# A gMLP and sliding-window-attention trunk: the first mixer's output projection in groups two to four as seven block products

## The chip, the cores and the metric

The kernel runs on one core of a Trainium2 chip. The metric is device time of one launch in microseconds (us); lower is better. PE is the tensor engine (TensorE), DVE is VectorE, ACT is ScalarE, POOL is GpSimd and SP is SyncE, which issues nearly all transfers.

## The reference, cut to what matters

```
def mixer_a(h, w_in, ln_g, ln_b, w_s, b_s, w_out):
    u, v, z = jnp.split(h @ w_in, 3, axis=-1)          # h: 2048 x 1024, w_in: 1024 x 6144
    u = jax.nn.gelu(u)
    v = layer_norm(jax.nn.gelu(v), ln_g, ln_b)
    ...                                                 # v mixed over 128 positions, per group of 256 channels
    y = u * mixed.reshape(B, S, A_WIDTH) * jax.nn.silu(z)
    return y @ w_out                                    # y: 2048 x 2048, w_out: 2048 x 1024
...
x = x + gate * mixer_a(...)                             # then one layer of windowed attention, and a final norm
```

All is fp32. The text is about `y @ w_out`.

## The kernel before

Tokens are worked in four groups of T = 512 (`NG`, index i = 0 to 3; "group two" is i = 1). A group's part of the first mixer runs on PE in three stretches: the v columns, eight u/z stages (`GROUPS`, index g; each two units, the spatial matmuls of L2130 and four transposes of the group before), and the output projection. After the four groups comes the attention layer, in slots.

A matmul in fp32 is made of three in a rounded type (`split3`, L1930 to L1932): every operand is a rounded part and a remainder. A unit is a weight block of 4 row tiles x 512 columns, loaded by SP in two halves into one of two buffers in turn, or a third (`buffers`, L147). ScalarE rounds each half (`hi`, L1117, into `w_hi`), GpSimd subtracts (`lo`, L935, into `w_lo`). In groups two to four the v columns are already done as seven block products instead of eight (`FACTORS`, `v_blocks`), with four of the seven weight factors combined beforehand: in group one SP loads the four blocks (`load_comb`, L684), VectorE forms four sums (`comb`, L1600), ScalarE and GpSimd split them (L1140, L954), and SP stores both parts (`keep_comb`, L691), read back later as they are (`kept_split`).

The projection (`ao_unit`) has 8 units per group, each of 8 pieces: 4 token tiles x 2 pairs of rows. The y tiles are rounded by ScalarE (`y_round`, L1273) and their remainders taken by VectorE (`y_rest`, L1736); all eight PSUM banks accumulate until `a_residual` (L1588, L1590) multiplies by the gate and adds to x1. In the last unit PE also turns the next group's x (`x_transposes`).

Each engine runs its own list in the order written, with semaphore waits; nothing is reordered. The order that matters around the change is SP's: `a_stage(i, q)` with q = 4 + g issues the loads of u/z stage g, stores the split weights of two stages earlier (`keep_split`), stores a combination, loads the next and the next B weights to be split (`load_split`); after it `keep_turned` stores two turned tiles of x1. ScalarE's `turned_round` (L1180) waits for the store of the tile before. ScalarE's list in a stage is: `turned_round`, `v_norm` (L1284), `hi` of the next stage's first unit, u and z activations, `hi` of its second unit, split, combination. GpSimd's is: `lo` of both units, split, combination.

## Time and profile before

| | us |
|---|---|
| median of 3 runs | 2280.02 (2278.74 to 2284.73) |
| the profiled execution | 2281.42 |
| its span | 2279.3 |
| PE busy in the span | 2207.7 |
| granted PE clock, mean | 0.994 |

How to read the rows: times are us from the span's start. A line of the timeline gives start, duration, engine and source line, output<-inputs and the count merged; in brackets the idle time before it and what ended it. SPq is SP's own queue of DMA issues: there the duration is that of issuing, not of the transfer. Matmul durations overlap, so their spacing is their cost.

### The profile page before, as it was taken

The numbers are of one execution on the slowest core, as the hardware profiler recorded it, in microseconds if no ns is written. First come the engines' busy times: TensorE is split into PE (matmuls) and PEld (weight loads), VectorE is DVE, ScalarE is ACT, GpSimd is POOL, SyncE is SP. The second block draws the span as 40 slices with busy tenths as digits, with TensorE's granted clock in tenths as the row PEclk, the third lists the DMA queues.
The fourth block names the chain that finished last, engine by engine and source line by source line (L and its number), as shares of the span: only waits on it lengthen the run. The fifth ranks groups of instructions, "written<-read, shape, count | busy, mean of one in ns | idle before, by whom it ended". The sixth has DMA issues, their size and how long they took to land.

```text
span 2279.3 us, 28527 instructions
## 1 busy us (share of the span) xinstructions
PE 2207.7 (97%) x10582; PEld 1850.2 (81%) x10582; DVE 1266.7 (56%) x1691; ACT 969.9 (43%) x1854; POOL 991.4 (43%) x628
## 2 busy tenths in 40 slices
PE   4999999999999999999999999998999999999998
PEld 4788877888888878888888888786888888887886
DVE  5848864453634534554345653436767657656754
ACT  4334453534444444444353445323444434433442
POOL 2447775555544475454474455420222232232222
PEclk9999999999999999999999999999999999999999
DMA  8656785584556394566476455768686797786654
GB/s 332 241 200 234 269 301 182 202 297 152 194 208 226 122 344 153 181 214 241 135 264 230 163 206 194 260 233 306 231 308 219 279 340 242 263 310 237 218 202 166
DMA packets 226474, 529.90 MB, mean 232 GB/s; under 512 B 19009, under 2 KB 94881, under 8 KB 225953
## 3 DMA queue, kind: packets, MB, share of 16 engines
q1 hardware_dynamic: 223376, 522.79, 64.2%
q10 hardware_dynamic: 2960, 5.30, 0.7%
q8 instruction: 84, 1.38, 0.2%
q14 instruction: 54, 0.43, 0.1%
HBM read 411.62 MB, written 106.95 MB: 228 GB/s over the span
## 4 chain that ended last, share of the span: by engine, by line
PE 80%; DMA 7%; DVE 4%; POOL 3%; ACT 2%; POOLq 1%; issue 1%; DVEq 1%; SPq 1%; ACTq 0%
PE ps L1930 24%; PE ps L1932 24%; PE ps L1931 23%; DMA w_raw<-in_a_w_out 2%; PE ps L2130 2%; DMA w_raw<-in_a_w_in 2%; POOL w_lo L935 2%; DVE acc L1491 1%; PE ps L2168 1%; PE ps L2169 1%; PE ps L2194 1%; DMA b_input<-hbs 1%; ACT w_hi L1117 1%; PE ps L2203 1%; PE ps L2204 1%
## 5 line engine op out<-in xcount | busy, mean ns | idle before, releaser
L935 POOL TENSOR_TENSOR w_lo<-w_raw,w_hi 128x1024 fp32r<-128x1024 f32 x244 | 621.3, 2561 | 664.4 <-ACT w_hi L1117 664.0
L1117 ACT ACTIVATE w_hi<-w_raw 128x1024 fp32r<-128x1024 f32 x244 | 257.6, 1059 | 577.8 <-DMA w_raw<-in_a_w_in 364.9
L1930 PE MATMUL ps<-h,w_hi 128*128 128x512 f32 x1024 | 402.0, 393 | 1.3 <-DVE wz L1715 0.8
L1932 PE MATMUL ps<-h,w_lo 128*128 128x512 f32 x1024 | 398.8, 389 | 0.0
L1931 PE MATMUL ps<-h,w_hi 128*128 128x512 f32 x1024 | 398.5, 389 | 0.0
L1066 POOL TENSOR_SCALAR_AFFINE_SELECT pt<-pt 128x512 fp32r<-128x512 f32 x128 | 82.4, 643 | 396.0 <-ACT pt L1422 343.3
L1930 PEld LDWEIGHTS ps<-h,w_hi 128*128 128x128 f32 x1024 | 192.3, 188 | 41.7 <-POOL w_lo L935 1.3
L1932 PEld LDWEIGHTS ps<-h,w_lo 128*128 128x128 f32 x1024 | 192.2, 188 | 40.5
L1931 PEld LDWEIGHTS ps<-h,w_hi 128*128 128x128 f32 x1024 | 192.3, 188 | 39.4 <-issue 0.2
L1930 PE MATMUL ps<-w_hi,y_hl 128*128 128x512 f32 x512 | 203.4, 397 | 7.7 <-POOL w_lo L935 5.7
L1932 PE MATMUL ps<-w_hi,y_hl 128*128 128x512 f32 x512 | 200.8, 392 | 0.0
L1931 PE MATMUL ps<-w_lo,y_hl 128*128 128x512 f32 x512 | 200.5, 392 | 0.0
L1930 PE MATMUL ps<-r,w_hi 128*128 128x512 f32 x480 | 192.8, 402 | 0.0
L1931 PE MATMUL ps<-r,w_hi 128*128 128x512 f32 x480 | 188.4, 393 | 0.0
L1932 PE MATMUL ps<-r,w_lo 128*128 128x512 f32 x480 | 188.3, 392 | 0.0
L1736 DVE TENSOR_TENSOR y_hl<-vy,y_hl 128x512 fp32r<-128x512 f32 x64 | 89.5, 1456 | 176.8 <-ACT y_hl L1273 176.5
L1715 DVE SCALAR_TENSOR_TENSOR wz<-wz,ps 128x512 f32<-128x512 f32 x64 | 43.4, 685 | 173.7 <-ACT wz L1303 173.6
L1930 PE MATMUL ps<-w_hi,r 128*128 128x512 f32 (+1 forms) x352 | 125.8, 357 | 4.7 <-DVE x L1815 1.6
L1075 POOL TENSOR_TENSOR pp<-pp,rden 128x512 f32<-128x512 f32 x64 | 72.1, 1126 | 131.6 <-DVE rden L1903 131.6
L1932 PE MATMUL ps<-w_hi,r 128*128 128x512 f32 (+1 forms) x352 | 123.5, 351 | 0.0
L1931 PE MATMUL ps<-w_lo,r 128*128 128x512 f32 (+1 forms) x352 | 123.5, 351 | 0.0
L1930 PEld LDWEIGHTS ps<-w_hi,y_hl 128*128 128x128 f32 x512 | 96.9, 189 | 28.8 <-issue 7.3
(249 smaller groups left out, 4455.7 us busy)
## 6 DMA issues: line engine op xcount, KB each, us to landing
w_raw<-in_a_w_in SPq DMA_DIRECT2D x256, 256.0 KB, 3.5
w_hi<-b_weights_split SPq DMA_DIRECT2D x104, 512.0 KB, 4.3
w_lo<-b_weights_split SPq DMA_DIRECT2D x104, 512.0 KB, 5.9
w_raw<-in_a_w_out SPq DMA_DIRECT2D x64, 512.0 KB, 4.4
w_raw<-in_a_w_in SPq DMA_DIRECT2D x52, 512.0 KB, 5.8
w_hi<-v_weights_combined SPq DMA_DIRECT2D x48, 512.0 KB, 4.5
w_lo<-v_weights_combined SPq DMA_DIRECT2D x48, 512.0 KB, 6.1
kv_input<-xks SPq DMA_DIRECT2D x32, 512.0 KB, 6.8
```

Source lines behind the costliest of these rows:

```text
L935: g.tensor_tensor(wlo[p][:, rows_], raw[p][:, rows_], whi[p][:, rows_].bitcast(F32), ALU.subtract).then_inc(w_lo, 1)
L1066: last = g.affine_select(out=pt[:, 2 + m].rearrange("p (h q) -> p h q", h=4), in_=pt[:, m].rearrange("p (h q) -> p h q", h=4), compare_op= ...
L1075: g.tensor_tensor(p4, p4, rden[:, a % 2, :, None].broadcast_to([P, 4, P]), ALU.mult) \
L1117: s_.activation(whi[p][:, rows_], raw[p][:, rows_], ACT.Copy).then_inc(w_hi, 1)
L1491: v.scalar_tensor_tensor(there, rows_, sc[:, kt:kt + 1], there, ALU.mult, ALU.add).then_inc(ada_used, 1)
L1715: v.scalar_tensor_tensor(wz[:, ft, :], wz[:, ft, :], 1.0, bank(2 + ft), ALU.add, ALU.mult) \
L1736: v.tensor_tensor(y[:, t % 4, 1, :], vy[:, T * t:T * t + T], y[:, t % 4, 0, :].bitcast(F32), ALU.subtract).then_inc(y_lo, 1)
L1930: t_.matmul(dst_, stat[0], mov[0], start=start, stop=False)
L1931: t_.matmul(dst_, stat[0], mov[1], start=False, stop=False)
L1932: return t_.matmul(dst_, stat[1], mov[0], start=False, stop=stop)
L2130: last = t_.matmul(bank(4 + ft, P, P * cnk), vs[:, cnk, P * ft:P * ft + P], wst[:, g, :], start=True, stop=True)
L2168: t_.matmul(dst_, q, ks[:, kh, 0, P * blk:P * blk + 2 * P], start=True, stop=False)
```

## The change

The projection of groups two to four becomes seven block products. The tokens are halved (first and second 256 of the group), the 16 row tiles of `w_out` are halved into even and odd ones, and the columns into two of 512. Each product m has two halves q (rows 4q to 4q+3 of the pairs), a unit of 4 pieces each, in `OUT_ORDER`. GpSimd forms the combined y factors (`y_sums`), ScalarE rounds factors (`factor_round`), VectorE takes their remainders (`factor_rest`) and also the weight remainders of product 2 (`weights_rest`). Products 0 and 1 are copied out of PSUM (`out_keep`), the others added by VectorE (`out_add`, `out_done`), and `take_up` does what `a_residual` did.

The combined weights of `w_out` are eight combinations (two even/odd halves per pair of tiles, four factors; factors 0 and 2 stored split, 1 and 3 stored whole). One is formed in group one, at stage 3; seven in group two, in stages 4 to 10, that is in u/z stages g = 0 to 6. Their buffers are the places 0 and 2 in turn. In group two `keep_comb` of stage q - 1 stands in `a_stage` behind the stage's second unit and ahead of `load_comb`; `combs_kept(1)` waits for all stores before the first projection unit. A fourth weight buffer lies in the place of x. The loads of the rope table and the final norm move behind the last group.

```diff
+OUT_FACTORS = [("T", 2), ("B", 0, 0), ("T", 1), ("B", 1, 0), ("T", 0), ("T", 3), ("B", 1, 1)]
+OUT_ORDER = [(0, 0), (1, 0), (0, 1), (1, 1)] + [(m, q) for m in range(2, PRODUCTS) for q in range(2)]
+KEPT_WHOLE = (1, 3)
+OUT_BANK = (0, 2, 4, 6, 0, 4, 6)
...
+COMBS = [(0, 3, "a", 0, 1)] + [(0, 4 + c, "v", c, c % 3) for c in range(8)] \
+    + [(1, 3 + c, "a", c, (2, 0)[c % 2]) for c in range(1, 8)]
+COMB_PLACE = [comb[4] for comb in COMBS]
...
+                if i == 1:
+                    sp.wait_ge(piece_done, pieces(v_unit(1, V_UNITS[1] - 1), 4))
+                    sp.wait_ge(block_sum, sums(1, 1, 16))
+                col = WIDTH + 1024 * (n // 4)
...
             def keep_comb(c):
-                m, sv, kt = COMB_PLACE[c], c // 4, c % 4
+                _, _, whose, n, m = COMBS[c]
                 sp.wait_ge(comb_lo, c + 1)
+                to, some = (cad[:, n // 4] if whose == "a" else cbd[n // 4]), rounded_combs(c)
                 for part, w in ((0, cbh[m]), (1, cbl[m])):
-                    sp.dma_start(cbd[sv, :, kt // 2, part, :, kt % 2].rearrange("t p n -> p t n"), w[:].bitcast(F32)) \
+                    sp.dma_start(to[some, n % 4 // 2, part, :, n % 2].rearrange("t p n -> p t n"),
+                                 w[:, some].bitcast(F32)).then_inc(comb_out[m], 16)
+                if whose == "a":
+                    sp.dma_start(to[1:4:2, n % 4 // 2, 0, :, n % 2].rearrange("t p n -> p t n"), cbr[m][:, 1:4:2]) \
...
+            def combs_kept(i):
+                for m in range(3):
+                    sp.wait_ge(comb_out[m], combs_out(i, m))
             def a_stage(i, q):
                 first = uz_unit(i, 0, 0) - 8
+                if i == 1 and q == 12:
+                    combs_kept(1)
                 if q >= 1:
                     unit(first + 2 * q)
                 s = split_at(i, q - 2)
                 if s is not None:
                     keep_split(s)
-                for c in combs_at(i, q - 2):
-                    keep_comb(c)
+                if i == 0:
+                    for c in combs_at(i, q - 2):
+                        keep_comb(c)
                 if q >= 1:
                     unit(first + 2 * q + 1)
+                if i == 1:
+                    for c in combs_at(i, q - 1):
+                        keep_comb(c)
                 for c in combs_at(i, q):
                     load_comb(c)
                 s = split_at(i, q)
...
+                for n in range(2, 16):
+                    unit(ao_first(i) + n)
+                    if n == 4:
                         keep_turned(i - 1, GROUPS - 1)
-                    if i == NG - 1 and n == 3:
-                        for part in range(3):
-                            load_xk(0, part)
-                    if i == NG - 1 and n == 8:
-
-                        sp.wait_ge(piece_done, pieces(ao_unit(i, 2, 1), 8))
...
+            sp.wait_ge(ao_read, at("ao_read", NG - 1, 4))
...
+            def y_sums(i, s, q):
+                even0, even1, odd0, odd1 = y_block(0, 0, q), y_block(1, 0, q), y_block(0, 1, q), y_block(1, 1, q)
+                pool.drain()
+                if s == 3:
+                    pool.wait_ge(y_done, at("y_done", i, 4 * q + 4))
+                    pool.wait_ge(piece_done, pieces(ao_block(i, 0, q), 4))
+                    there, a, op, b = y_factor(2, q), even0, ALU.subtract, even1
+                elif s == 1:
+                    there, a, op, b = even1, even1, ALU.add, odd1
+                elif s == 2:
+                    pool.wait_ge(y_lo, y_half(i, 4, q))
+                    there, a, op, b = even1, even1, ALU.subtract, even0
+                else:
+                    pool.wait_ge(y_lo, y_half(i, 3, q))
+                    there, a, op, b = odd0, odd0, ALU.subtract, even1
+                g.tensor_tensor(there, a, b, op).then_inc(y_sum, 1)
             def rstd(dst_, src, tmp, signal):
                 pool.nop(nofuse=True)
...
+                else:
+                    y_sums(i, 3, 0)
+                    lo(ao_block(i, 1, 1))
+                    y_sums(i, 3, 1)
+                    y_sums(i, 1, 0)
+                    y_sums(i, 1, 1)
+                    lo(ao_block(i, 3, 0))
+                    lo(ao_block(i, 3, 1))
+                    for s in (2, 4):
+                        y_sums(i, s, 0)
+                        y_sums(i, s, 1)
+                    if i < NG - 1:
                         x_stage(i + 1)
-                    lo(ao_unit(i, 0, n))
+                    for m in (5, 6):
+                        lo(ao_block(i, m, 0))
+                        lo(ao_block(i, m, 1))
                 if i == NG - 1:
...
+                    factor_round(0, 1)
                     turned_round(i - 1, GROUPS - 1, 7)
-                hi(ao_unit(i, 1, 0))
-                hi(ao_unit(i, 1, 1))
-                y_round(2)
-                hi(ao_unit(i, 2, 0))
-                hi(ao_unit(i, 2, 1))
-                y_round(3)
-                if i < NG - 1:
-                    x_squares(i + 1)
-                hi(ao_unit(i, 3, 0))
-                hi(ao_unit(i, 3, 1))
+                    factor_round(1, 1)
+                    factor_round(2, 0)
+                    hi(ao_block(i, 1, 1))
+                    hi(ao_block(i, 2, 0))
+                    out_keep(0)
+                    factor_round(2, 1)
+                    hi(ao_block(i, 2, 1), (0,))
+                    out_keep(1)
+                    hi(ao_block(i, 2, 1), (1,))
+                    for q in range(2):
+                        factor_round(3, q)
+                    for q in range(2):
+                        hi(ao_block(i, 3, q))
+                    for q in range(2):
+                        factor_round(4, q)
...
+                def factor_rest(m, q):
+                    dve.drain()
+                    dve.wait_ge(y_hi, y_half(i, m, q))
+                    there = yb[m % 2][:, 4 * q:4 * q + 4]
+                    v.tensor_tensor(there[:, :, 1, :], y_factor(m, q), there[:, :, 0, :].bitcast(F32), ALU.subtract) \
+                        .then_inc(y_lo, 1)
+                def weights_rest(u):
+                    p = BUFFER[u]
+                    for hh in range(2):
+                        rows_ = slice(2 * hh, 2 * hh + 2)
+                        dve.wait_ge(w_hi, 2 * SPLIT_HERE[u] + hh + 1)
+                        v.tensor_tensor(wlo[p][:, rows_], raw[p][:, rows_], whi[p][:, rows_].bitcast(F32),
+                                        ALU.subtract).then_inc(w_lo2, 1)
...
+                def out_add(m, c, there, base):
+                    product = out_there(m, c)
+                    dve.drain()
+                    v.tensor_tensor(there[:, c, :], base[:, c, :], product, ALU.add).then_inc(out_sum, 1)
+                def out_done(m, c, base, n, cnk):
+                    product = out_there(m, c)
+                    dve.drain()
+                    v.tensor_tensor(product, base[:, c, :], product, ALU.add)
+                    take_up(i, n, cnk, product)
...
+                    factor_rest(0, 0)
+                    factor_rest(1, 0)
+                    uz_group(GROUPS - 1)
+                    factor_rest(0, 1)
                     turned_rest(i - 1, GROUPS - 1, 7)
-                y_rest(2)
-                y_rest(3)
-                if i < NG - 1:
-                    x_scale(i + 1)
-                dve.wait_ge(x1_in, at("x1_in", i, 16))
-                dve.nop(nofuse=True)
-                for cnk in range(NC):
-                    a_residual(i, 0, cnk)
-                for cnk in range(NC):
+                    factor_rest(1, 1)
+                    factor_rest(2, 0)
+                    weights_rest(ao_block(i, 2, 0))
+                    factor_rest(2, 1)
+                    for c in range(2):
+                        dve.wait_ge(out_kept, out_kepts(i, c + 3))
+                        out_add(1, c, up, up)
+                    weights_rest(ao_block(i, 2, 1))
+                    factor_rest(3, 0)
+                    factor_rest(3, 1)
+                    factor_rest(4, 0)
+                    dve.wait_ge(xk_out[0], 16 * KT * i)
+                    for c in range(2):
+                        out_add(2, c, up, up)
+                        out_add(2, c, ue, ut)
+                    factor_rest(4, 1)
+                    dve.wait_ge(x1_in, at("x1_in", i, 16))
+                    dve.nop(nofuse=True)
+                    for c in range(2):
+                        out_done(3, c, ut, 0, c)
+                    factor_rest(5, 0)
+                    factor_rest(5, 1)
                     if i < NG - 1:
-                        h_rest(i + 1, 2 * cnk)
-                        h_rest(i + 1, 2 * cnk + 1)
-                    a_residual(i, 1, cnk)
+                        x_scale(i + 1)
+                    factor_rest(6, 0)
+                    for c in range(2):
+                        out_add(4, c, ue, ue)
+                        out_add(4, c, ut, ut)
+                    factor_rest(6, 1)
+                    for c in range(2):
+                        out_add(5, c, ut, ut)
+                        out_add(5, c, ue, ue)
+                    for c in range(2):
+                        out_done(5, c, up, 0, 2 + c)
+                        if i < NG - 1:
+                            h_rest(i + 1, 2 * c)
+                            h_rest(i + 1, 2 * c + 1)
+                    if i < NG - 1:
+                        h_rest(i + 1, 4)
+                        h_rest(i + 1, 5)
+                    for c in range(2):
+                        out_done(6, c, ut, 1, c)
+                        if i < NG - 1:
+                            h_rest(i + 1, 6 + c)
+                    for c in range(2):
+                        take_up(i, 1, 2 + c, ue[:, c, :])
...
+                def project_blocks():
...
-                        unit(u, token(u, 4 * n, lambda k: y_hl[ku % 2][:, k], ku == 0, ku == 3),
-                             bank_free if ku == 0 else None,
-                             next_x if ku == 3 and n == 1 and i < NG - 1 else None)
+                            x_transposes(i + 1, 4 * q + k)
+                        pe.wait_ge(y_lo, y_half(i, m, q))
+                        unit(u, token(u, OUT_BANK[m], lambda k: yb[m % 2][:, 4 * q + k], q == 0, q == 1),
+                             bank_free if q == 0 else None, next_x if m == 6 and i < NG - 1 else None)
```

## Rows read from the trace of the kernel before

**Rows 1.** the page's busy times, share of the span and instruction counts

```profile
PE 2207.7 (97%) x10582; PEld 1850.2 (81%) x10582; DVE 1266.7 (56%) x1691; ACT 969.9 (43%) x1854; POOL 991.4 (43%) x628
```

**Rows 2.** windows: us, busy (count) of PE, PEld, DVE, ACT, POOL; clock, DMA share, GB/s

```profile
510.40:702.40 192.00, 192.00 (x928) 161.68 (x927) 90.39 (x97) 90.56 (x128) 98.17 (x41) 1.00 0.52 179
702.60:794.80 92.20, 91.83 (x422) 75.77 (x421) 47.10 (x46) 39.03 (x53) 40.91 (x18) 1.00 0.51 181
1428.00:1517.40 89.40, 87.25 (x386) 71.91 (x385) 32.75 (x35) 25.36 (x33) 36.04 (x17) 1.00 0.61 223
142.00:333.30 191.30, 189.97 (x898) 158.33 (x896) 139.12 (x101) 90.24 (x115) 135.19 (x53) 1.00 0.72 250
```

**Rows 3.** timeline of PE in group two's projection: start, us, instruction

```profile
712.30 0.39 PE L1930 MATMUL ps<-w_hi,y_hl 128*128 128x512 f32 x1
...
713.66 0.39 PE L1930 MATMUL ps<-w_hi,y_hl 128*128 128x512 f32 x1
```

**Rows 4.** timeline of PE, ends of u/z stages seven and eight of group two

```profile
676.47 1.95 PE L2130 MATMUL ps<-wst,vs 128*128 128x128 f32 x16
...
700.51 1.95 PE L2130 MATMUL ps<-wst,vs 128*128 128x128 f32 x16
```

**Rows 5.** timeline of POOL behind those two ends

```profile
681.27 5.47 POOL L935 TENSOR_TENSOR w_lo<-w_raw,w_hi 128x1024 fp32r<-128x1024 f32 x2 [7.47 <-ACT w_hi L1117]
686.70 2.40 POOL L945 TENSOR_TENSOR wsl<-wsr,wsh 128x1024 fp32r<-128x1024 f32 x1
...
705.85 5.76 POOL L935 TENSOR_TENSOR w_lo<-w_raw,w_hi 128x1024 fp32r<-128x1024 f32 x2 [8.13 <-ACT w_hi L1117]
```

**Rows 6.** timeline of SP's queue over the same time

```profile
684.38 5.82 SPq L644 DMA_DIRECT2D w_raw<-in_a_w_out  x2
...
700.70 0.90 SPq L644 DMA_DIRECT2D w_raw<-in_a_w_out  x2
...
703.36 0.83 SPq L731 DMA_DIRECT2D xs<-in_x  x1
704.24 1.69 SPq L811 DMA_DIRECT2D x<-in_x  x1
...
708.41 5.81 SPq L644 DMA_DIRECT2D w_raw<-in_a_w_out  x2
```

**Rows 7.** timeline of ACT; in brackets idle time before and what ended it

```profile
685.46 0.69 ACT L1187 ACTIVATE xks<-ps,vec 128x512 fp32r<-128x512 f32 x1 [0.60 <-DMA b_input<-hbs]
686.05 0.77 ACT L1188 ACTIVATE hbs<-ps,sb,gb 128x512 fp32r<-128x512 f32 x1
686.71 2.07 ACT L1284 ACTIVATE vs<-vy,v_nm,v_rs 128x256 f32<-128x256 f32 x4
...
721.39 1.06 ACT L1117 ACTIVATE w_hi<-w_raw 128x1024 fp32r<-128x1024 f32 x1 [10.79 <-DMA w_raw<-in_a_w_out]
```

**Rows 8.** windows inside two bursts of transfers, columns as in rows 2

```profile
232.90:241.70 8.80, 8.80 (x49) 7.58 (x48) 6.23 (x8) 0.66 (x2) 4.30 (x2) 1.00 1.01 327
707.00:717.00 10.00, 10.00 (x46) 8.29 (x45) 9.05 (x8) 3.52 (x7) 4.61 (x2) 1.00 1.02 400
```

**Rows 9.** timeline of POOL and SP, a combination in group one

```profile
226.41 5.65 POOL L954 TENSOR_TENSOR cbl<-cbr,cbh 128x1024 fp32r<-128x1024 f32 x2
...
232.09 0.37 SPq L691 DMA_DIRECT2D v_weights_combined<-cbh  x1
```

**Rows 10.** tile y_hl: ns min/median/max, first and last start; then timeline of DVE

```profile
L1736 DVE TENSOR_TENSOR y_hl<-vy,y_hl x64: 677/681/2901, 325.4 to 1482.8; 128x512 fp32r<-128x512 f32 x64
...
703.69 1.23 DVE L1718 TENSOR_TENSOR wz<-wz,gu 128x1024 f32<-128x1024 f32 x1
```

**Rows 11.** timeline of PE at the start of group one's projection

```profile
335.33 0.50 PE L1930 MATMUL ps<-w_hi,y_hl 128*128 128x512 f32 x1 [2.02 <-DVE y_hl L1736]
...
336.37 0.63 PE L1930 MATMUL ps<-w_hi,y_hl 128*128 128x512 f32 x1
336.80 0.63 PE L1931 MATMUL ps<-w_lo,y_hl 128*128 128x512 f32 x1
```

More of the change, by code:

```diff
@@ L2157, in logits @@
+                if i == 0:
+                    project()
+                else:
+                    project_blocks()
             def logits(a):
```

359 lines of the change are left out of this document (262 added, 97 removed).

## The prediction

> **What bounds the kernel now.** I read the page's busy shares first: PE is busy for 2207.7 of 2279.3 us [rows 1]. No other engine comes near it, so time falls only if PE gets fewer instructions without getting new gaps. The table by stretches says where PE is dense: in group two the stretch of the u/z stages has PE busy for 192.00 of 192.00 us with DMA at 0.52, and the projections of groups two and four have gaps of 0.4 and 2.2 us [rows 2]. Inside a projection matmuls start every (713.66 - 712.30)/6 = 0.227 us [rows 3]; the printed 0.39 us is the length of one with its overlap.
>
> **Matmuls removed.** A projection has 8 units of 8 pieces of 6 matmuls, 384. The new one has 14 units of 4 pieces of 6, 336. Three groups lose 144 x 0.227 = 32.6 us if nothing else binds.
>
> **The shared queue in group two (the term that decides).** Between u/z stages g-1 and g, `a_stage` now makes SP wait in `keep_comb` for `comb_lo` of the combination formed in stage g-1, and only after that come the loads of the weights of stage g+1. Count from the end E of PE's stage g-1. Stages are 700.51 - 676.47 = 24.0 us apart [rows 4]. GpSimd forms that remainder last: after E the two halves of the unit just loaded end at 686.74, E + 10.3, the split of a B weight is 2.4 us more, to E + 12.6 [rows 5], and the combination's remainder is one more instruction of that size: E + 15. Today SP issues the first half for stage g+1 at 684.38, E + 7.9 [rows 6]. After the change it is queued behind three stores, two loads of the combination, one load to be split and the two turned tiles of `keep_turned`: 8 x 0.52 = 4.2 MB.
>
> What such a pile costs is shown by the x loads: from 700.70 on, 1.05 MB of weights, 1.05 MB of turned tiles and 4.2 MB of x lie ahead of a weight half issued at 708.41, and ScalarE gets it at 721.39 after 10.79 us idle [rows 6, 7]. That is 6.8 MB in 20.7 us, 330 GB/s with start-up. In the middle of a burst DMA moves 400 GB/s in large packets and 327 with the combinations' [rows 8]. So 4.2 MB take 12.7 us; bounds 10.5 and 13.
>
> The chain then closes on itself. ScalarE's `turned_round` of the next stage waits until the turned tiles behind those 4.2 MB are stored; in order behind it come that copy (0.69 + 0.77 us), `v_norm` (2.07) and the rounding of the weight half (1.06) [rows 7]; then GpSimd's four halves, split and combination, 6 x 2.4 = 14.4 us, after which SP is released again. 12.7 + 4.6 + 14.4 = 31.7 us against a stage of 24.0, and each combination instruction that meets VectorE's work is 2.8 instead of 2.4 us [rows 9], so up to 34.3. I take 32.5: 8.5 us of PE idle per stage, bounds 6.5 and 10.5. Seven combinations are formed, in u/z stages 1 to 7. The first pile has no turned tiles and costs 3 us (bounds 1, 5), five full rounds cost 42, and at the end the wait for all combinations (`combs_kept(1)`) in front of the first projection unit, plus the late `v_norm`, costs 6 (3, 8). Sum +51 us, bounds +36 and +65. Behind SP's wait stand the unit loads, `keep_split` and the x1 tiles; nobody else waits on SP. VectorE's four sums per combination (0.7 us each) fall into that idle time.
>
> The Trainium skill, page "DMA: Bandwidth & Descriptors", section "Specifications", gives a limit of about 358 GB/s for HBM per core. By it the pile would take an estimated 11.7 us. The trace of this kernel exceeds that figure, 400 GB/s [rows 8], so I keep the row; the difference is 1 us per stage and changes no sign.
>
> **The same combinations in group one.** There the queue keeps its old order (`keep_comb` two stages later, ahead of the unit that PE needs last, at 232.09 [rows 9]), and PE is busy for 189.97 of 191.30 us with eight combinations under it [rows 2]. The ninth, at stage 3, puts 2.8 us of VectorE sums and 1 MB in front of the last adaLN rows. VectorE waits there anyway; +1 us (0, 2).
>
> **The projections themselves, groups two to four.** VectorE and GpSimd exclude each other when both read SBUF: a VectorE remainder of 512 columns takes 681 ns at the median and 2901 at most, a product of 1024 columns 1.23 undisturbed [rows 10]. In the new projection almost all of it is of this kind. From 9 us after its start (end of the first own-split unit) GpSimd has 8 `y_sums` and 14 halves, 22 x 2.4 = 52.8 us, VectorE 12 factor remainders and 4 weight halves, 16 x 1.2 = 19.6 us, and x scaling with its rstd some 4 us. In a row that is 9 + 76 = 85 us before the last half is there, 2.7 us more for what PE does with it: 88. Hand-overs overlap by some 0.1 us each, 22 of them, so 86, against 76.2 + 2.4 (transposes) for PE alone, and against 92.2 today [rows 2]. Group four has no x work: 82.5 against 89.4. Followed in order, the gaps lie at the second half of the first own-split unit, at (2, 1), whose remainder stands behind two output sums in VectorE's queue (2.6 us), and from (5, 0) on. Gains 6, 6 and 7, less 1 to 2 each for the longer tail (`out_done` is three VectorE instructions before the last `h_rest`): -15 us in all. Bounds: -4, if every hand-over costs the full contended difference, and -24, if the transfers above stretch the group so that the port has time. The matmuls' full 32.6 us are out of reach.
>
> The Trainium skill, page "SBUF — State Buffer", section "Who interferes with whom", says that the pair of ports which VectorE and GpSimd share is an exclusive lock for a whole instruction, taken by the first to issue. That speaks against this change; with a mere sharing of bandwidth the projection would be bound by PE, and the term an estimated -28. The rows (2901 against 681 ns) show the wait of a whole instruction, so -15 stays.
>
> **Clock.** After a gap of 2 us matmuls start 0.43 us apart for some time, the lower of the two levels, 1.2 against 2.4 GHz [rows 11]; nine such starts cost 1.8 us. In the u/z stages this lies within the loop above, where PE isn't last; I add nothing.
>
> **Sum.** Profiled execution 2281.4 us (span 2279.3 and 2.1 around it), median of the runs 2280.0, 1.4 lower. 2281.4 + 51 + 1 - 15 = 2318.4, less 1.4: 2317 us. Own range: 2280 + 36 + 0 - 24 = 2292 to 2280 + 65 + 2 - 4 = 2343.
>
> **Rivals.** (1) Faster: SP's wait is harmless, because the next weights reach GpSimd before the stage ends. It has 24.0 + 2.1 us after E; SP is free at E + 15, and one half alone, with rounding and remainder, needs 7.6 us (700.70 to 708.3 [rows 5, 6]). With nothing ahead of it that is E + 22.6, in time. It decides for faster if the pile ahead is under 3.5 us, 1.2 MB. Against it stand 4.2 MB and the x loads' row. Then 2280 + 1 - 15 = 2266, range 2253 to 2274. Chance 0.10. (2) About the same: piles are drained but the turned tiles land early, so that the loop is 6 + 4.6 + 14.4 = 25 us; 10 us in all: 2280 + 10 + 1 - 15 = 2276, range 2270 to 2290. Chance 0.13. (3) Slower still: VectorE's combination sums and remainders hold the port in every stage (all six GpSimd instructions at 2.8, SP's issue slowed by a full queue), loop 37 us, and the projections gain nothing: 2280 + 75 = 2355, 2343 to 2370. Chance 0.07. My forecast has 0.70. The range goes from 2274 to 2345: it leaves out the faster case and most of (3). A measurement tells 0.3%, 6.8 us, from no change: faster 0.12, same 0.09, slower 0.79.
>
> **What would show it.** Right: group two's u/z stretch grows from 192 to about 240 us, with GpSimd or "issue" and DMA as releasers of PE's wait, `w_hi` of the first half waiting for `in_a_w_in` by over 8 us, stores of `a_weights_combined` right after the last GpSimd instruction of a stage, DMA idle before and full after; groups three and four unchanged there at 192, and projections at 82 to 88 us. Wrong: if that stretch stays under 200 us the queue step fell; if the projections take 80 us or less, the port step did; over 92, its bound.

## The result and the profile after

The changed kernel takes 2348.56 us, median of 4 runs (2347.42 to 2352.43), against 2281.09 us before: ratio 1.0297, 95% interval 1.0279 to 1.0316. It is slower, as forecast, but by 67 us instead of 37. 2348.6 lies above the stated range, whose upper end was 2345, and inside that of rival 3 (2343 to 2370).

The page's busy line of the changed kernel (columns as in [rows 1]) and two of its slices:

```profile
PE 2199.3 (94%) x10438; PEld 1835.6 (78%) x10438; DVE 1421.8 (61%) x1789; ACT 1008.5 (43%) x1880; POOL 1121.1 (48%) x660
...
PE   5999999998768889999989999999899999999998
...
PEclk9999999999888999999999999999999999999999
```

PE has its 144 matmuls less, as the diff says. But its busy time fell by only 8.4 us, where 32.6 would go with the matmuls: part of those left run at the lower clock. The loss stands in slices 10 to 14 (58.7 us each, 528 to 821 us), above all in 11 to 13: group two's u/z stages. The table by stretches says it in numbers (columns as in [rows 2]). The first row is of the kernel before: the way from the end of group two's projection to the next group's first u/z stage. The others are of the changed kernel: group two's u/z stages two to eight, its projection, the way to the next group; the same pair in group three; group four's projection.

```profile
794.00:894.90 100.90, 99.11 (x437) 81.08 (x436) 44.33 (x63) 42.52 (x62) 63.45 (x37) 1.00 0.73 258
```

```profile
532.20:773.00 240.80, 184.99 (x814) 153.75 (x812) 112.36 (x101) 81.17 (x115) 113.90 (x40) 0.88 0.59 206
773.60:863.20 89.60, 83.73 (x367) 66.18 (x366) 77.48 (x58) 51.46 (x62) 74.64 (x28) 0.98 0.84 308
863.20:970.70 107.50, 101.75 (x437) 83.20 (x436) 54.52 (x77) 42.66 (x62) 65.64 (x37) 0.97 0.67 234
1141.00:1226.40 85.40, 81.84 (x368) 66.96 (x367) 74.04 (x53) 49.97 (x61) 75.07 (x28) 0.98 0.82 293
1226.40:1335.10 108.70, 102.50 (x438) 83.68 (x437) 55.97 (x78) 42.70 (x62) 65.56 (x37) 0.97 0.66 232
1505.40:1587.00 81.60, 77.77 (x340) 62.84 (x339) 59.74 (x51) 34.06 (x37) 69.34 (x24) 1.00 0.92 340
```

Cut at the same matmuls in both traces, the difference of 67.1 us in the last matmul's start is made of these parts:

| stretch | before | after | difference | forecast |
|---|---|---|---|---|
| start to group two's first u/z stage | 532.3 | 530.3 | -2.0 | +1 |
| group two, u/z stages two to eight, and the step to the projection | 170.4 | 243.3 | +73.0 | +51 |
| projections of groups two, three, four | 90.9, 91.5, 89.4 | 89.3, 85.0, 81.3 | -1.6, -6.5, -8.1 | -6, -6, -7 |
| from the projection to the next group's first u/z stage | 101.3, 100.9 | 107.8, 109.0 | +6.5, +8.1 | +1 to 2 each |
| u/z stages of groups three and four | 170.4 each | 170.4 each | 0 | 0 |
| last projection to the end | 753.6 | 751.3 | -2.3 | 0 |

The first and the last row can't be told from the spread of one kernel's traces: in the runs below that have the same code up to there, group two's first u/z stage starts its spatial matmuls at 527.5 to 534.2, and the last row is 750.0 to 758.9.

Two things are to be explained: why the u/z stages of group two lost 73 us, and why the 16.2 us that the projections gained were given back, all but 1.6 us, in the stretch behind them.

**One round of group two.** Timelines of the changed kernel, in the form of [rows 5 to 7]: SP's release in the round before, GpSimd's last remainder and SP's queue behind it; ScalarE; PE; GpSimd and VectorE; SP again.

```profile
576.38 0.37 SPq L825 DMA_DIRECT2D a_weights_combined<-cbh  x1
...
610.11 2.38 POOL L1116 TENSOR_TENSOR cbl<-cbr,cbh 128x1024 fp32r<-128x1024 f32 x1
...
612.52 0.37 SPq L825 DMA_DIRECT2D a_weights_combined<-cbh  x1
...
618.67 0.43 SPq L907 DMA_DIRECT2D b_input<-hbs  x1
```

```profile
626.89 0.69 ACT L1389 ACTIVATE xks<-ps,vec 128x512 fp32r<-128x512 f32 x1 [24.60 <-DMA b_input<-hbs]
...
628.14 2.07 ACT L1512 ACTIVATE vs<-vy,v_nm,v_rs 128x256 f32<-128x256 f32 x4
630.10 2.00 ACT L1318 ACTIVATE w_hi<-w_raw 128x1024 fp32r<-128x1024 f32 x2
```

```profile
630.26 3.65 PE L2473 MATMUL ps<-wst,vs 128*128 128x128 f32 x16 [9.03 <-ACT vs L1512]
```

```profile
631.23 11.88 POOL L1097 TENSOR_TENSOR w_lo<-w_raw,w_hi 128x1024 fp32r<-128x1024 f32 x4 [18.74 <-ACT w_hi L1318]
643.07 3.37 POOL L1107 TENSOR_TENSOR wsl<-wsr,wsh 128x1024 fp32r<-128x1024 f32 x1
646.40 2.57 POOL L1116 TENSOR_TENSOR cbl<-cbr,cbh 128x1024 fp32r<-128x1024 f32 x1
```

```profile
631.97 2.71 DVE L1860 TENSOR_TENSOR cbr<-cbr 128x512 f32<-128x512 f32 x1
634.75 2.74 DVE L1862 TENSOR_TENSOR cbr<-cbr 128x512 f32<-128x512 f32 x1
...
638.78 2.06 DVE L1976 TENSOR_TENSOR wz<-wz,gu 128x1024 f32<-128x1024 f32 x1
```

```profile
649.00 0.37 SPq L825 DMA_DIRECT2D a_weights_combined<-cbh  x1
```

One round goes like this. The remainder `cbl` ends at 612.49, and SP issues the three stores at once (612.52). `b_input<-hbs`, the last of the pile, is issued at 618.67, and ScalarE gets its landing at 626.89: 14.4 us after the release. ScalarE's copies and `v_norm` take 3.2 us, the rounding of the weight half 1.1; GpSimd's six instructions run from 631.23 to 648.97, 17.7 us, without a gap; and SP stores again at 649.00. 14.4 + 3.2 + 1.1 + 17.7 = 36.4 us. PE needs 24.0 of them and is idle for 9.0 in one piece; of the rest 1.7 us are the 16 spatial matmuls behind it, at the lower clock (3.65 us against 1.95 in [rows 4]). The first round is shorter: SP is released at 545.30, then at 576.38, 612.52 and 649.00, and for the last time at 757.74.

### The profile page after: what moved, and what is told of

It is laid out like the page before. It is cut to its first block and busy times, and to the rows that moved or that the text cites. A ratio compares the mean times of both kernels' runs of the same rounds, so it can differ in the third digit from the quotient of the medians.

```text
span 2346.4 us, 28747 instructions
## 1 busy us (share of the span) xinstructions
PE 2199.3 (94%) x10438; PEld 1835.6 (78%) x10438; DVE 1421.8 (61%) x1789; ACT 1008.5 (43%) x1880; POOL 1121.1 (48%) x660
## 5 line engine op out<-in xcount | busy, mean ns | idle before, releaser
L1097 POOL TENSOR_TENSOR w_lo<-w_raw,w_hi 128x1024 fp32r<-128x1024 f32 x244 | 653.7, 2699 | 608.2 <-ACT w_hi L1318 607.9
L1318 ACT ACTIVATE w_hi<-w_raw 128x1024 fp32r<-128x1024 f32 x256 | 268.2, 1058 | 447.0 <-DMA w_raw<-in_a_w_in 351.4
L2270 PE MATMUL ps<-w_hi,yb 128*128 128x512 f32 x336 | 135.3, 403 | 13.3 <-issue 6.5
L2271 PE MATMUL ps<-w_lo,yb 128*128 128x512 f32 x336 | 132.3, 394 | 0.0
L2272 PE MATMUL ps<-w_hi,yb 128*128 128x512 f32 x336 | 132.2, 394 | 0.0
L2270 PE MATMUL ps<-w_hi,h 128*128 128x512 f32 x272 | 111.4, 410 | 17.2 <-DVE h L1776 14.8
L1818 DVE SCALAR_TENSOR_TENSOR xks<-ps,vec,xks 128x512 fp32r<-128x512 f32 x32 | 23.9, 747 | 158.2 <-ACT hbs L1390 158.2
```

The lines of the kernel that those rows point to most:

```text
L1097: g.tensor_tensor(wlo[p][:, rows_], raw[p][:, rows_], whi[p][:, rows_].bitcast(F32), ALU.subtract).then_inc(w_lo, 1)
L1318: s_.activation(whi[p][:, rows_], raw[p][:, rows_], ACT.Copy).then_inc(w_hi, 1)
L1818: v.scalar_tensor_tensor(xks[m][:, 1, :], bank(b), vec[:, ROW_KVN + kt:ROW_KVN + kt + 1], xks[m][:, 0, :].bitcast(F32), ALU.mult, ALU.subt ...
L2270: t_.matmul(dst_, stat[0], mov[0], start=start, stop=False)
L2271: t_.matmul(dst_, stat[0], mov[1], start=False, stop=False)
L2272: return t_.matmul(dst_, stat[1], mov[0], start=False, stop=stop)
```

## Experiments

The diffs show the lines that matter; `...` marks lines left out.

**1. Only the place of the store in SP's queue.**

```diff
...
-                if i == 0:
-                    for c in combs_at(i, q - 2):
-                        keep_comb(c)
+                for c in combs_at(i, q - 2):
+                    keep_comb(c)
                 if q >= 1:
                     unit(first + 2 * q + 1)
-                if i == 1:
-                    for c in combs_at(i, q - 1):
-                        keep_comb(c)
...
```

The lines left out move the wait for all stores (`combs_kept(1)`) from ahead of the first projection unit to ahead of the third; the first two wait for all but the last store of each buffer.

> The changed kernel, with the store of a combination in group two back where group one has it: two stages later, behind the store of the split weights and ahead of the stage's second unit; the last wait for all stores goes ahead of the third projection unit. Theory A (SP waits for the combination of the stage before, and the next weights queue behind a 4.2 MB pile; round 36.3 us against 24.0): every one of the seven combinations is still formed, but group two's u/z stretch goes back from 240.8 us (end of its first spatial matmuls to the end of its last) to 168 to 172, and the time from 2348.6 to 2274 to 2282. Rival B (the combinations' own transfers, VectorE sums and GpSimd remainders fill the stage whatever the order): stretch above 200, time above 2308.

Measured: 2277.25 us, ratio to the kernel before 0.9977 (0.9966 to 0.9987). The same stretch, a window of this run, and its queue:

```profile
533.20:701.90 168.70, 168.49 (x813) 141.34 (x812) 125.20 (x106) 83.89 (x115) 104.02 (x40) 1.00 0.85 298
```

```profile
641.59 0.37 SPq L766 DMA_DIRECT2D w_raw<-in_a_w_in  x1
...
644.82 0.37 SPq L825 DMA_DIRECT2D a_weights_combined<-cbh  x1
...
652.47 0.37 SPq L766 DMA_DIRECT2D w_raw<-in_a_w_in  x1
...
654.48 0.88 SPq L817 DMA_DIRECT2D cbr<-in_a_w_out  x2
```

All seven combinations are still loaded, formed, split and stored. The DMA share is 0.85 and PE is busy for 168.49 of 168.70 us. The weights of the next stage now go out ahead of the stores (641.59), the other unit between them and the next loads. So the place of the store is worth 71 us (2348.56 against 2277.25); rival B falls. The edit changes that place in two ways: the store stands ahead of the stage's second unit instead of behind it, and one stage later. No run separates the two, here or in experiment 5.

**2. Without the seven combinations.** `COMBS` loses its last seven entries, so they are neither loaded, formed nor stored; the loads of the projection read `v_weights_combined`.

> The changed kernel without the seven combinations of group two: they are neither loaded, formed nor stored, and the projection reads as many bytes of other combined weights (that work is left out, the rest is the same). Theory A: stretch 168.2 us as before the change, time 2270 to 2278; the difference to the run with the old order of the queue is what the combinations cost when nothing waits for them, 0 to 5 us. Rival B: this run is under 2280, the other stays above 2308. Both: the projections stay at 85 to 90, 85 and 81.5 us.

Measured: 2272.00 us, ratio 0.9956 (0.9941 to 0.9972); stages two to eight, with the step to the projection, 170.4 us as before the change. In the right order of the queue the combinations cost 5 us between the runs' medians (2277.25 and 2272.00), of which the traces show 0.7 in the u/z stages and 2.8 in group two's projection (88.0 against 85.2).

**3. The turned tiles ahead of the wait.** The late store stays.

```diff
                 if i == 1:
+                    if q >= 6:
+                        keep_turned(0, q - 6)
                     for c in combs_at(i, q - 1):
                         keep_comb(c)
...
-                    if i >= 1 and g >= 2:
+                    if i >= 2 and g >= 2:
                         keep_turned(i - 1, g - 2)
```

> The changed kernel (store of the combination still in its late place), with the stores of the turned x1 tiles in group two issued ahead of the wait for the combination instead of behind. Theory A with its parts (36.3 us = 14.4 from release to the landing of the turned tiles, 3.2 ScalarE's copies and v_norm, 1.1 rounding, 17.6 GpSimd's six instructions): ScalarE no longer waits for that store, and the raw weights land after 3.3 MB instead of 4.2 MB; round 30 to 32 us, u/z stretch 240.8 - 5 x 5 = 212 to 220 us, time 2320 to 2328. Rival Q (the raw weights behind the same pile are what counts, the turned tiles are not in the chain): round 34 to 36.3, time 2338 or more.

Measured: 2320.49 us, ratio 1.0160 (1.0139 to 1.0180). Two releases in a row, and ScalarE between them:

```profile
606.63 0.37 SPq L825 DMA_DIRECT2D a_weights_combined<-cbh  x1
...
637.17 0.37 SPq L825 DMA_DIRECT2D a_weights_combined<-cbh  x1
```

```profile
619.56 1.06 ACT L1320 ACTIVATE w_hi<-w_raw 128x1024 fp32r<-128x1024 f32 x1 [16.41 <-DMA w_raw<-in_a_w_in]
```

The round is 30.5 us: ScalarE now rounds the weight half 12.9 us after the release, where it took 17.6 with the turned tiles, `v_norm` and all. Of the 5.9 us that a round lost, 3.2 are ScalarE's copies and `v_norm`, which no longer stand behind the landing; 1.5 the earlier landing, with 3.1 MB instead of 4.2 ahead of the weights; 1.2 GpSimd, whose part took 16.5 us. Time and round came inside the stated numbers, and rival Q falls: the store of the tiles was in the chain, as the prediction had it. Stages two to eight with the step were 210.0 us, and group two's projection got longer, 92.6 us against 89.3.

**4. Smaller stores.** The three stores of a combination carry 64 of 512 columns, `w[:, some, 0:64]`; the rest of each is left out, and the projection reads other stored weights.

> The changed kernel with its late store, but the three stores of a combination in group two carry 64 of 512 columns, and the projection reads other stored weights (that work is left out). The pile behind SP's wait shrinks from 4.2 to 2.8 MB. Theory A (the bytes ahead of the turned tiles set the first 14.4 us of a round of 36.3): 1.38 MB less at the 291 GB/s of that stretch, 4.7 us less per round, round 31 to 32.5 us, u/z stretch 240.8 - 5 x 4.7 = 213 to 220 us, time 2320 to 2328. Rival R (the round is set by SP's issuing and by the engines' chain, bytes don't matter): round 35 to 36.3, time 2342 or more.

Measured: 2332.52 us, ratio 1.0226 (1.0205 to 1.0246). Releases in a row and ScalarE:

```profile
608.05 0.37 SPq L826 DMA_DIRECT2D a_weights_combined<-cbh  x1
...
641.88 0.37 SPq L826 DMA_DIRECT2D a_weights_combined<-cbh  x1
```

```profile
619.81 0.69 ACT L1391 ACTIVATE xks<-ps,vec 128x512 fp32r<-128x512 f32 x1 [21.95 <-DMA b_input<-hbs]
```

The round is 33.8 us, the pile 11.8 instead of 14.4. The sign was right and rival R falls, but round and time lie outside the stated numbers: 2.6 us per round came back where 4.7 were expected. The edit shortens rows from 2 KB to 256 B and leaves their number as it was, and SP still issues every transfer (in the changed kernel 6.2 us pass from the release to the issue of `b_input`). Which of these kept the other 2.1 us is not shown.

**5. The same store moved in the kernel before.** In group one:

```diff
-                for c in combs_at(i, q - 2):
-                    keep_comb(c)
                 if q >= 1:
                     unit(first + 2 * q + 1)
+                for c in combs_at(i, q - 1):
+                    keep_comb(c)
...
-                            keep_comb(len(COMB_STAGES) - 1)
```

The last line is the store of the last combination, which stood in the projection and now lies in the moved loop; nothing is added or left out.

> The kernel before the change with one line moved: in group one the combinations of the v weights are stored one stage later than they are formed, behind the stage's second unit, as the changed kernel does in group two, instead of two stages later and ahead of it. Nothing is added or left out. Theory A (a property of that place in SP's queue, not of the change's weights): after each release come 2.1 MB of stores, 1.05 of loads and 0.5 of a weight to be split, then the raw half: 3.9 MB at 291 GB/s is 13.5 us, 1.1 rounding, 17.6 GpSimd; round 32 us against 23.6, seven of them: u/z stretch of group one 191 + 50 to 60, time 2330 to 2345. Rival S (the changed kernel's round is long because of the turned tiles or of the port, which group one has not or has already): stretch under 215, time under 2305.

Measured: 2359.44 us, ratio 1.0342 (1.0321 to 1.0362). Group one's u/z stages two to eight before (first row) and in this run, then one round of this run:

```profile
166.10:333.30 167.20, 165.87 (x785) 138.26 (x783) 132.25 (x85) 81.74 (x103) 124.44 (x47) 1.00 0.76 264
```

```profile
164.30:389.30 225.00, 177.78 (x786) 147.30 (x785) 78.34 (x81) 73.56 (x93) 117.53 (x45) 0.89 0.56 189
```

```profile
207.62 0.37 SPq L691 DMA_DIRECT2D v_weights_combined<-cbh  x1
...
222.94 1.06 ACT L1116 ACTIVATE w_hi<-w_raw 128x1024 fp32r<-128x1024 f32 x1 [22.96 <-DMA w_raw<-in_a_w_in]
...
224.08 11.37 POOL L934 TENSOR_TENSOR w_lo<-w_raw,w_hi 128x1024 fp32r<-128x1024 f32 x4 [16.49 <-ACT w_hi L1116]
...
237.75 4.74 POOL L953 TENSOR_TENSOR cbl<-cbr,cbh 128x1024 fp32r<-128x1024 f32 x2
242.52 0.37 SPq L691 DMA_DIRECT2D v_weights_combined<-cbh  x1
```

The moved store costs the kernel before 79 us. The round has the same three parts (15.3 to the weights, 1.1, 18.4 for GpSimd, which here has seven instructions), 34.9 us, longer than the 32 that I expected, and the time lies above the 2330 to 2345 expected; the stretch grew by 57.8 us, inside the 50 to 60, and the rest is in the step to the projection (12.2 us against 2.0) and in the projection (106.1 against 95.9), behind the last combination. Rival S falls: neither the turned tiles nor the new weights are needed.

**6. VectorE's list at the end of the projection.**

```diff
+                        for kt in range(4):
+                            h_rest(i + 1, kt)
                         for c in range(2):
                             out_done(5, c, up, 0, 2 + c)
-                            h_rest(i + 1, 2 * c)
-                            h_rest(i + 1, 2 * c + 1)
-                        h_rest(i + 1, 4)
-                        h_rest(i + 1, 5)
+                        for kt in range(4, 8):
+                            h_rest(i + 1, kt)
                         for c in range(2):
                             out_done(6, c, ut, 1, c)
-                            h_rest(i + 1, 6 + c)
```

> The changed kernel, VectorE's list at the end of the projection reordered: the first four remainders of the next group's h ahead of the last two output sums of product five, the other four ahead of product six's. Theory C (the 6.4 and 8.1 us that the way from the end of the projection to the next group's u/z stages is longer than before come from VectorE's list: 3.8 us of wait for the fourth remainder, a second wait for the copy behind product six's sums, and matmuls at half the clock behind each): that way falls from 107.6 and 108.8 us to 101 to 103 in groups three and four, time 2348.6 - 10 = 2334 to 2342. Rival D (VectorE and GpSimd hold the shared port there, so the order doesn't matter): within 2 us of 2348.6.

Measured: 2350.25 us, ratio 1.0306 (1.0284 to 1.0328), no gain; the way to the next group fell by 0.8 and 2.1 us only. The time is rival D's. What the edit was to mend stands in the changed kernel's rows, PE and VectorE at the end of group two's projection, then ScalarE's copy of the next group's first product:

```profile
867.24 0.80 PE L2270 MATMUL ps<-w_hi,h 128*128 128x512 f32 x1 [3.50 <-DVE h L1776]
```

```profile
864.76 5.79 DVE L1776 TENSOR_TENSOR h<-hfw,h 128x512 fp32r<-128x512 f32 x4
```

```profile
876.12 1.09 ACT L1440 ACTIVATE ut<-ps 128x512 f32<-128x512 f32 x2 [7.13 <-DVE x L1843]
```

And what the edit made of it:

```profile
1232.09 6.73 DVE L1776 TENSOR_TENSOR h<-hfw,h 128x512 fp32r<-128x512 f32 x4
```

```profile
1238.87 0.79 PE L2268 MATMUL ps<-w_hi,h 128*128 128x512 f32 x1 [4.10 <-DVE h L1776]
```

PE started the next group without a wait and stood 5.4 us later, ahead of its second product, which needs remainders five to eight. These now fell into GpSimd's shifted sums, 1.68 us each instead of 0.7. The wait had moved, at full price. That the order is worth nothing, as rival D has it, is refuted by the next run.

**7. A third order of the same list**, on top of experiment 1: `h_rest` 0 to 4, `out_done(6, 0)`, `h_rest` 5 and 6, `out_done(6, 1)`, `h_rest` 7, then `out_done(5, 0)` and `(5, 1)`; ScalarE's copy waits for the fourth sum instead of the sixth.

> The run with the old order of the queue, and VectorE's list at the end of the projection in a third order: four remainders of h ahead of the output sums as in the tail run, then the sums of product six in between the other four remainders, those of product five last, so that ScalarE's copy of the next group's first product waits for fewer of them. In the tail run PE started the next group without a wait and then lost 4.5 us at the fifth remainder, since remainders five to eight fell into GpSimd's shifted sums of h (1.7 us each instead of 0.7). Theory C2 (order and overlap both matter): way to the next group 103 to 105 us instead of 108.9 and 107.9, time 2277.3 - 9 = 2266 to 2271. Rival D (port time only moves): over 106, time 2274 to 2280.

Measured: 2270.26 us, ratio 0.9933 (0.9907 to 0.9958). Its way from group two's projection to the next group:

```profile
786.10:889.80 103.70, 99.65 (x440) 81.33 (x439) 54.71 (x77) 42.90 (x63) 66.07 (x37) 1.00 0.69 244
```

108.9 and 107.9 us became 103.7 and 104.9. The order is worth 5.2 and 3.0 us of some 7, and time and way came as theory C2 had them; a copy and some remainders still wait.

**8. GpSimd's order in the projection**, with both edits above (that of experiment 6): `x_stage` and the remainders of product five ahead of the sums of y for factor six.

> Both edits together, and GpSimd's list in the projection reordered as well: the rstd of x and the remainders of product five ahead of the last two sums of y. Theories A, C and E (the 3.0 us gap ahead of product five comes from GpSimd's order, not from its load): u/z stretch of group two 168 to 172, way to the next group 101 to 103, projections of groups two and three 82 to 84 us instead of 89.6 and 85.3; time 2255 to 2264, under the kernel before by 17 to 26 us. If A alone holds: 2274 to 2282. If the port binds the projections (each hand-over at full price), they stay at 85 and the time at 2262 to 2272.

Measured: 2287.59 us, ratio 1.0020 (1.0006 to 1.0033). The time expected was 2255 to 2264. The queue held (stages two to eight with the step 170.4 us), the way to the next group fell to 104.4 and 103.9 us, but the projections got longer: 93.7, 90.5 and 87.9 us. The gap ahead of product five went, but ScalarE's `factor_round(6, 0)` stands ahead of the rounding of product five's second half and waits for the sum of y that was now late. In group three PE waited 2.4 us for product five's second half, then for product six:

```profile
1146.62 0.77 PE L2268 MATMUL ps<-w_hi,yb 128*128 128x512 f32 x1 [3.77 <-issue]
```

Theory E falls as a remedy: it looked at one engine's list where three are interlocked.

**9. Who forms the weight remainders.** On top of experiment 1, `rest_by_vector` says which product's are VectorE's (2 in the changed kernel).

> The run with the old order of the queue, and the weight remainders of product two moved back from VectorE to GpSimd. Theory P: 4.8 us more of port time in each of three groups; projections 3 to 5 us longer (88 to 93, 88 to 90, 84 to 86), time 2286 to 2292. Rival V: VectorE is relieved where PE waited for it (the 1.3 us gap in product two), projections the same or shorter, time 2270 to 2278.

> The run with the old order of the queue, and the weight remainders of product five formed by VectorE (1.23 us undisturbed) instead of GpSimd (2.4). Theory P (VectorE and GpSimd exclude each other, their sum sets the projection's length): four remainders give back 4 x 1.2 us of port time, of which PE gaps can give some 3 to 5: projections 82 to 84, 81 to 83 and 78 to 79 us instead of 88.0, 85.1 and 80.8; time 2264 to 2271. Rival V (VectorE, in order, is the engine that comes last): projections as long or longer, time 2276 or more.

Measured with none: 2298.73 us, ratio 1.0061 (1.0042 to 1.0080). With products two and five: 2273.93 us, 0.9946 (0.9927 to 0.9965). Group three's projection, of experiment 1, of none, and of two and five:

```profile
1069.70:1154.80 85.10, 80.66 (x366) 65.22 (x365) 73.55 (x53) 49.60 (x60) 74.67 (x28) 1.00 0.81 293
```

```profile
1080.10:1171.90 91.80, 82.46 (x367) 66.31 (x365) 64.23 (x49) 49.76 (x60) 82.19 (x32) 0.96 0.76 272
```

```profile
1062.10:1150.50 88.40, 82.86 (x366) 67.38 (x365) 74.72 (x62) 49.52 (x60) 64.23 (x24) 0.96 0.78 281
```

With 88.0, 85.1 and 80.8 us in experiment 1, groups two to four take 94.3, 91.8 and 86.5 with none, and 84.1, 88.4 and 78.5 with two and five. Four remainders put on GpSimd lengthen each projection by 5.7 to 6.7 us, more than the 4.8 of theory P, and the time lies above its 2286 to 2292. Four taken away shorten those of groups two and four by 3.9 and 2.3 us, and lengthen group three's by 3.3: there the second half's remainders stood behind the scaling of x in VectorE's list and met GpSimd's next ones, 3.4 us each, where in group two they took 1.2 us each, ahead of GpSimd's. So rival V is right in group three; the time of this run lies between the two forecasts. The way to the next group is 5 us shorter in that run (103.8 and 103.1 against 108.9 and 107.9), which I had not expected of it.

**10. The remedy that these pointed to**: on top of experiment 7, VectorE takes only the first half of product five, and half of product two's second unit goes ahead of two sums.

> The run with the old order of the queue and VectorE's third order at the end, and in the projection VectorE takes the weight remainders of the first half of product five from GpSimd (the half for which PE waited 3.0 us), and the first half of those of product two's second unit ahead of the two output sums. Unlike the run with both halves of product five on VectorE, GpSimd keeps the second, which there stood behind the scaling of x and met GpSimd's next remainders (3.4 us each). Theory P: projections 81 to 84, 80 to 82 and 77 to 79 us instead of 87.7, 85.1 and 80.6, time 2254 to 2262, under the kernel before by 1.0 to 1.3%. Rival V (VectorE comes last): projections as in the run with the third order alone, 2266 to 2274.

Measured: 2277.14 us, ratio 0.9973 (0.9964 to 0.9983). Projections 90.8, 89.1 and 80.1 us: theory P's numbers missed in all three groups, and in groups two and three the projections are longer than in experiment 7 (87.7 and 85.1). The time lies above rival V's 2274 too. VectorE and PE in group three; the last row is VectorE's scaling of x in experiment 7:

```profile
1127.98 11.26 DVE L1758 TENSOR_SCALAR xs<-xs,x_rs 128x1024 f32<-128x1024 f32 x4
1139.34 3.19 DVE L2001 TENSOR_TENSOR yb<-vy,yb 128x1024 fp32r<-128x1024 f32 x1
```

```profile
1142.58 0.80 PE L2273 MATMUL ps<-w_hi,yb 128*128 128x512 f32 x1 [5.28 <-DVE yb L2001]
```

```profile
1116.16 11.23 DVE L1759 TENSOR_SCALAR xs<-xs,x_rs 128x1024 f32<-128x1024 f32 x4 [1.25 <-POOL x_rs L1167]
```

The scaling of x met GpSimd's remainders in experiment 7 too, 2.8 us each for 0.75. Counted from the start of the projection it came 2.6 us later (58.8 us against 56.2), behind the remainders of product five that VectorE had taken over, and the factor of product six came later with it.

**11. Less for GpSimd, same order.** On top of experiment 7, the sums of y for factors four and six work on 32 of 256 tokens.

> The run with VectorE's third order, and GpSimd's sums of y for factors four and six work on 32 of 256 tokens (the rest of that work is left out; all instructions, waits and orders stay). GpSimd then has some 9 us less to do in each projection. Theory P (GpSimd's time plus what it waits at the port is what the projection's end hangs on): projections 82 to 84, 80 to 82 and 77 to 79 us instead of 87.7, 85.1 and 80.6 (PE alone needs 78.7), time 2270.3 - 13 = 2253 to 2261. Rival V (VectorE's or ScalarE's own list, or the weights' transfers, come last): 84 or more in group three, time 2266 or more.

Measured: 2263.83 us, ratio 0.9926 (0.9909 to 0.9943). Projections of groups three and four:

```profile
1068.20:1148.70 80.50, 79.57 (x366) 65.60 (x365) 71.08 (x53) 49.52 (x60) 66.38 (x28) 1.00 0.85 308
1424.30:1504.70 80.40, 77.38 (x338) 62.51 (x337) 55.41 (x51) 33.95 (x37) 60.38 (x24) 1.00 0.92 343
```

Group three falls from 85.0 to 80.5 us, as theory P said. Groups two and four don't move (87.7 to 88.2, 80.6 to 80.5) with 8 us less GpSimd work. There its total is not what comes last, as rival V has it. In group two the trace shows PE's two long waits, both for VectorE: 2.9 us for the weight remainders of product two (2.3 in experiment 7), and 2.6 for the factor of product six (0.9), which VectorE finishes 73.9 us after the projection's start, no earlier than the 73.4 of experiment 7:

```profile
778.54 0.50 PE L2274 MATMUL ps<-w_hi,yb 128*128 128x512 f32 x1 [2.64 <-DVE yb L2004]
```

The time lies between theory P's (2253 to 2261) and rival V's (2266 or more).

## Why the prediction was right and wrong

**Sign and place: right.** The deciding term was the one named, SP's wait in `keep_comb`, in group two alone; groups three and four stayed at 170.4 us, and stores follow the last GpSimd instruction at once. Experiments 1 and 5 show it from both sides. Three signs came otherwise than foretold. PE's releaser is ScalarE's `v_norm`, which stands behind `turned_round`, and not GpSimd. ScalarE's long wait is for `b_input` (24.6 us), and `w_hi` of the first half has none. And the stretch of eight stages that was to grow from 192 to about 240 us became 265, by the table; the 240.8 above are stages two to eight alone.

**Size: wrong, in the length of a round.** This is the step that failed. I took 32.5 us, 12.7 + 4.6 + 14.4 and 0.8, with 34.5 as the upper bound; it is 36.3. Two terms were too small. The pile took 14.4 us, beyond my upper bound of 13: I priced it at the 330 GB/s of the x loads, while 4.2 MB in 14.4 us are 291 GB/s (the window shows 316 with what runs beside). And GpSimd's six instructions took 17.7 us, not 14.4; even six at 2.8 us, the price that I had for one that meets VectorE, are only 16.8. I had said that VectorE's sums "fall into that idle time". They do, for PE; but two of them meet GpSimd's remainders, and both pay (2.71 and 2.74 us for sums of 0.68, the first three remainders 2.8 to 2.9 instead of 2.4, 1.4 us together). The larger part, 2 us, I hadn't looked for: the fourth remainder and the split take 3.4 us each beside VectorE's y products (`wz<-wz,gu`, 2.06 us, and `vy<-wz,gu`, 1.76, where 1.23 is undisturbed) and a scaling of table values. In experiment 5 the sums are over before GpSimd starts, and two of its seven instructions still take 3.4 us. Of the miss of 3.8 us per round, 1.7 are the pile's and 3.3 GpSimd's, less 0.3 for ScalarE and the 0.8 of allowance. What made the pile slower than the x loads is not settled (experiment 4).

**Rival 3**, with a chance of 0.07, had the better loop: 37 us, all six GpSimd instructions slowed by VectorE, and projections that gain nothing. 2348.6 lies in its range, 6 us under its 2355. The projections did gain, and the tail took it back.

**Count: right; the first round was mis-sized.** I had a first pile of 3 us, five rounds of 8.5, and an end of 6. Between SP's seven releases lie one round of 31.1 us and five of 36.1 to 36.5: over 24.0 that is 7.0 and five times 12.2, and 4.8 of the 73.0 us are left for the end. So the first round cost 4 us more than foretold, the five 19 more, the end 1 less: the miss of 22. PE sees it shifted. Its spatial matmuls start at 530.3, 554.3, 594.0, 630.3, 666.6, 702.9, 739.2 and 769.7: nothing lost at first, since PE has a lead, then 15.6 us at once, four times 12.3, and 6.5.

**Projections: right to 3 us.** 16.2 us gained against 19 before the tail; 89.3, 85.0 and 81.3 us measured, 86, 86 and 82.5 foretold. That VectorE and GpSimd bind, not PE, is borne out by experiment 9 in all groups when work is added, and by 11 only in group three when it is taken away. The simple sum, port time in a row, gave nearly the right length, in part by luck, since it is not what comes last everywhere: experiment 10, designed from it, missed, and 11 moved one group of three.

The Trainium skill, page "SBUF — State Buffer", section "Who interferes with whom", calls the shared pair an exclusive lock held for a whole instruction. The rows agree: 3.4 us for either of a pair that takes 2.4 and 1.2 alone, and 0.69 us unchanged for sums with an operand in PSUM beside them.

**The tail: mis-sized, the second step that failed.** I gave 1 to 2 us to each group for the later end of VectorE's list; it was 6.5 and 8.1, some 11 us more in all. With the 22 of the u/z stages and the 3 of the projections, less the 5 of the table's first and last row, that is the miss of 30 but for rounding. I counted the three instructions ahead of the last `h_rest` and not that the late remainders run into GpSimd's sums of the next group, nor ScalarE's copy, which waits for product six's sums. Experiment 7 gets 5 and 3 us of it back.

**Clock: right for the loop, wrong for the tail.** In the u/z stages the slow matmuls lie inside the round, and the round sets the time. Behind the gap of 3.5 us in the tail of group two 11 matmuls start 0.43 us apart and cost about 2 us more, for which I had nothing.

**Rival 1** (faster, SP's wait harmless) gave 2266 us. With the store in the right place the kernel has 2277, with VectorE's third order 2270: with both edits the change is worth 0.7% (0.4 to 0.9), with the first alone 0.2% (0.1 to 0.3). Experiment 7 beats both kernels.

## What to carry to other kernels

When a store is put into an in-order queue of transfers, ask what is issued behind it and when that is needed: a wait for a result of this stage, ahead of the loads of the next, ties a whole stage into a loop (load, round, remainder, store), and the loop's length replaces PE's. Add up the loop with contended durations, and see the first turn as the one that eats the lead.

Work saved on PE is worth only what the last engine lets through; here half of 32.6 us, and nearly all of it was given back in the next stretch. Where three in-order lists are interlocked, moving an item by what one engine's gap shows failed in three edits of five (experiments 6, 8 and 10; 7 and, by 3 us, the second run of 9 gained); write down who waits for each item that is passed.

## What the runs showed that was not expected

A tuned kernel can stand one moved store away from a loss of 3.4% (experiment 5), with no byte and no instruction added. A VectorE instruction with one operand in SBUF and a scalar, the scaling of x, also waits for GpSimd: 11.26 us for four beside GpSimd's remainders (experiment 10; 11.30 in the changed kernel's group two), where one takes 0.75 while GpSimd is idle (experiment 9, two and five).
